# Chunked attention heads worked in eight steps of two chunks instead of sixteen of one

## The chip, the cores and the metric

One core of one Trainium2 chip runs the whole kernel. The metric is the device time of one execution in microseconds (us), the median of several runs. The profile was taken of one execution.

## The reference, cut to what matters

One layer on 1024 tokens of width 1024, all in float32:

```python
h = rmsnorm(x, pre_g)
p = h @ w_in                       # q, k, v, gate of group A and of group B
ya = sliding_window_sink_attention(aq, ak, av, sinks) * silu(ag)
yb = differential_attention(bq, bk, bv, lam, lambda_init, subln_g) * silu(bg)
y = concat(ya, yb) @ w_out
return x + rmsnorm(y, post_g)
```

Group A has 8 query heads and 2 key/value heads of 64. Tokens lie in 16 chunks of 64, and a chunk's queries see the keys of their own chunk and of the one before (64 queries by 128 keys). A linear bias in the distance is added, a learned sink takes part in the softmax, and the weights multiply the values. Group B has 4 heads with two softmax maps each; it is swept in blocks of 128 queries over all earlier keys, and the second map is subtracted with a factor before the values.

## The kernel before, in words

All order is written out by `make_schedule` (line 103). It makes one list of named steps, and each engine's program walks the list and does its own part of a step; so the place of a name in the list is the order on every engine's queue, and semaphores join the queues. After a preamble (normalise, transpose, project all values) the list is made of 51 slots: 24 units of group B (heads 0 to 2, eight query blocks each, unit names b0 to b23), 16 of group A (one for each chunk), the last 8 of B (b24 to b31), and 3 slots that finish. In a slot stand the scores of one unit and the transpose and values of an earlier one: one slot earlier for B, two for A (line 142). Between them stand pieces of the input projection. `PIECES_BESIDE` (line 85) says how many to a slot. A piece is 4 matmuls of 512 columns; six pieces make a half of a projection unit (128 output columns by 512 tokens). When a half is done, ACT stores it (`store`), and DVE makes what belongs to it: low parts for the q and k of B (`store_low`), the gate product (`gate`). Two units ahead of a unit's first piece, its weights are split (`split`): ACT writes the rounded part w_hi (line 711), POOL the rest w_lo (line 622). One piece is always taken behind the values (line 197), whatever the number says.

A chunk c goes through these steps. `a_scores` on PE (line 1228) is four matmuls, each for a pair of heads, on 64 rows of the array, into one of two sets of PSUM banks; on DVE (line 1044) four reductions that add the bias, write `a_weights` and take the row's minimum, then the sink's argument (line 1049); on ACT (line 820) four exponentials with row sums, then the sink's (line 823). `a_weights` on DVE (lines 1055, 1058) is the total and its reciprocal, on POOL (line 676) the multiply with it. `a_transpose` is four transposes on PE (line 1236) into the bank `turned`, which the B units use too, and ACT's copy (line 831). `a_values` is two matmuls on PE (line 1246), which fill half of the bank `mixed`, and DVE's scaled copy into `qT_A` (line 1063). The buffers `a_weights` hold two chunks and share their place with `weights_1` of B.

`SCORES_FIRST` and `PIECE_BETWEEN` (lines 89, 90) name slots in which the scores stand ahead of the transposes, or a piece between the two. In a B unit, DVE mixes the two maps (`b_mix`, line 1000), PE transposes (line 1194), ACT copies (line 792), PE multiplies with the values (line 1204).

Of the kernel before, what the change touches and what calls it, by code (L numbers as in the profile page):

```python
# [31 lines left out]
P = 128  # L32
# [12 lines left out]
CHUNKS = SEQ // CHUNK  # L45
HALF = 512
# [56 lines left out]
def make_schedule():  # L103
# [33 lines left out]
    order = [("b", u) for u in range(3 * TILES)] + [("a", c) for c in range(CHUNKS)]  # L137
# [3 lines left out]
    for unit, n in place.items():  # L141
        turns.setdefault(n + (1 if unit[0] == "b" else 2), []).insert(0, unit)
# [80 lines left out]
def hybrid_layer(nc, x, w_in, w_out, pre_norm_g, post_norm_g, sinks, lambda_q1, lambda_k1,  # L223
# [27 lines left out]
    a_weights = place("a_weights", 148.25, [P, 2, A_PAIRS, P])  # L251
    a_weightsT = place("a_weightsT", 152.25, [P, A_PAIRS, P])
# [15 lines left out]
    small = place("small", 206.25, [P, 352])  # L268
# [17 lines left out]
    def column(width):  # L286
        taken[0] += width
        assert taken[0] <= 352
        return small[:, taken[0] - width:taken[0]]
# [12 lines left out]
    min_a = column(2 * A_PAIRS)  # L302
    sum_a = column(2 * A_PAIRS)
    sink_arg = column(2 * A_PAIRS)
    sink_w = column(2 * A_PAIRS)
    total_a = column(2 * A_PAIRS)
    inv_a = column(2 * A_PAIRS)
# [110 lines left out]
    def a_scores_at(c, j):  # L418


        return 1024 * (c % 2) + 512 * (j // 2) + P * (j % 2)
# [112 lines left out]
    with nc.Block() as block:  # L534
# [83 lines left out]
        def _(pool):  # L618
# [35 lines left out]
            for step, *i in SCHEDULE:  # L654
# [16 lines left out]
                elif step == "a_weights":  # L671
                    c = i[0]
                    pool.wait_ge(a_inverted, c + 1)
                    w = a_weights[:, c % 2]
                    r = inv_a[:, 4 * (c % 2):4 * (c % 2) + 4].unsqueeze(2).to_broadcast([P, A_PAIRS, P])
# [7 lines left out]
        def _(act):  # L683
# [53 lines left out]
            for step, *i in SCHEDULE:  # L737
# [46 lines left out]
                elif step == "b_transpose":  # L784
# [4 lines left out]
                    if u == 3 * TILES:  # L789
                        act.wait_ge(a_valued, CHUNKS)  # L790
# [23 lines left out]
                elif step == "a_scores":  # L814
                    c = i[0]
                    s = 4 * (c % 2)
                    for j in range(A_PAIRS):
                        w = a_weights[:, c % 2, j, :]
                        act.wait_ge(a_biased, 4 * c + j + 1)
                        nc.scalar.activation(w, w, ACT.Exp, scale=-1.0, bias=min_a[:, s + j:s + j + 1],  # L820
                                             accum_out=sum_a[:, s + j:s + j + 1]).then_inc(a_exped, 1)
                    act.wait_ge(a_sinked, c + 1)
                    nc.scalar.activation(sink_w[:, s:s + 4], sink_arg[:, s:s + 4], ACT.Exp).then_inc(a_exped, 1)
                elif step == "a_transpose":
                    c = i[0]
                    if c:
                        act.wait_ge(a_valued, c)
# [3 lines left out]
                    nc.scalar.activation(a_weightsT[:, :, :], turned[:, :].rearrange("p (j q) -> p j q", q=P),  # L831
# [30 lines left out]
        def _(dve):  # L862
# [80 lines left out]
            for step, *i in SCHEDULE:  # L943
# [20 lines left out]
                elif step == "gate":  # L964
# [13 lines left out]
                    else:  # L978
                        dve.wait_ge(mixed_read, mixed_users.index(("a_values", CHUNKS - 1)) + 1)
# [22 lines left out]
                elif step == "b_scores":  # L1002
# [7 lines left out]
                    if u == 3 * TILES:  # L1010
                        dve.wait_ge(turned_full, turned_count("a_transpose", CHUNKS - 2))
                    if u == 3 * TILES + 2:
# [20 lines left out]
                elif step == "a_scores":  # L1033
                    c = i[0]
                    s = 4 * (c % 2)
                    if c == 0:
# [3 lines left out]
                    if c >= 2:  # L1040
                        dve.wait_ge(turned_full, turned_count("a_transpose", c - 2))
                    dve.wait_ge(a_scored, c + 1)
                    for j in range(A_PAIRS):
                        nc.vector.tensor_tensor_reduce(  # L1044
                            out=a_weights[:, c % 2, j, :], in0=scores[:, a_scores_at(c, j):a_scores_at(c, j) + P],
                            in1=dist_a[:, min(c, 1), :], scale=neg_slope[:, j:j + 1], scalar=neg_sink[:, j:j + 1],
                            op0=ALU.add, op1=ALU.min, accum_out=min_a[:, s + j:s + j + 1]).then_inc(a_biased, 1)
                    dve.wait_ge(a_biased, 4 * c + 4)
                    nc.vector.tensor_tensor(sink_arg[:, s:s + 4], min_a[:, s:s + 4], neg_sink,
                                            ALU.subtract).then_inc(a_sinked, 1)  # L1050
                elif step == "a_weights":
                    c = i[0]
                    s = 4 * (c % 2)
# [5 lines left out]
                elif step == "a_values":  # L1059
                    c = i[0]  # L1060
                    dve.wait_ge(a_valued, c + 1)

                    nc.vector.tensor_scalar(qT_A[:, :, c],
                                            mixed[:, 0:A_PAIRS * CHUNK].rearrange("p (r s q) -> p r s q", s=2, q=CHUNK),
# [34 lines left out]
        def _(pe):  # L1099
# [51 lines left out]
            for step, *i in SCHEDULE:  # L1151
# [63 lines left out]
                elif step == "a_scores":  # L1215
                    c = i[0]
                    if c == 0:
# [4 lines left out]
                    if c >= 2:  # L1222
                        pe.wait_ge(a_biased, A_PAIRS * (c - 1))
                    for j in range(A_PAIRS):
                        part = slice(HEAD_DIM * (j // 2), HEAD_DIM * (j // 2 + 1))
                        at = a_scores_at(c, j)
                        pair = qT_A[part, j % 2, c].rearrange("p s q -> p (s q)")
                        last = nc.tensor.matmul(scores[:, at:at + P], pair, kT_A[part, CHUNK * c:CHUNK * c + P],  # L1228
                                                start=True, stop=True)
                    last.then_inc(a_scored, 1)  # L1230
                elif step == "a_transpose":
# [3 lines left out]
                    for j in range(A_PAIRS):  # L1235
                        last = nc.tensor.transpose(turned[:, P * j:P * j + P], a_weights[:, c % 2, j, :],  # L1236
                                                   ident[:, :])
                    last.then_inc(turned_full, 1)
                elif step == "a_values":
                    c = i[0]  # L1240
                    pe.wait_ge(turned_read, turned_count("a_transpose", c))
                    pe.wait_ge(mixed_read, mixed_before((step, *i)))
                    for h in range(2):
                        part = slice(HEAD_DIM * h, HEAD_DIM * (h + 1))
                        v = v_sb[:, c // 2, B_WIDTH:V_WIDTH] if c % 2 else v_shift[:, c // 2, :]
                        last = nc.tensor.matmul(mixed[part, 0:A_PAIRS * CHUNK], v[:, part],  # L1246
                                                a_weightsT[:, 2 * h:2 * h + 2, :], start=True, stop=True)
# [37 lines left out]
```

## Time and profile before

| | |
|---|---|
| median of 3 runs | 531.47 us (531.39 to 532.06) |
| span of the profiled execution | 529.6 us |
| PE busy | 511.7 us (97%) |
| DVE busy | 269.9 us (51%) |
| ACT busy | 250.5 us (47%) |
| POOL busy | 105.8 us (20%) |
| mean granted clock of PE | 0.997 of full speed |

The span runs from the first to the last instruction; the profiled execution has no time of its own beside it, and the median of the runs is 1.87 us above it. Engines: PE is the matrix engine (its weight loads are listed as PEld), DVE the vector engine, ACT the scalar engine, POOL GpSimd. Lines such as L1164 are lines of the kernel. Matmuls are pipelined, so their printed lengths overlap; where the time of a group is wanted, it is read from its start to the start of the next.

### The profile page before, as it was taken

What the parts mean: (1) busy time and instruction counts of PE and PEld (TensorE: products, weight loads), DVE (VectorE), ACT (ScalarE), POOL (GpSimd) and SP (SyncE); (2) the same over time, 40 slices, a digit from 0 to 9 for tenths busy, and PEclk for the clock granted to TensorE, in tenths of its full rate; (3) what the DMA queues carried; (4) which work ended last, traced back from release to release, by engine and by line L of the source; (5) the groups of instructions that cost most, each with busy time, mean ns of one, the idle gap of its engine ahead of it and who ended that gap; (6) DMA issues with size and microseconds to landing.
All of it is one profiled execution on the core that took longest, in us unless ns stands there. A gap on an engine that the chain in (4) does not pass through costs nothing.

```text
span 529.6 us, 7514 instructions
## 1 busy us (share of the span) xinstructions
PE 511.7 (97%) x2776; PEld 424.8 (80%) x2776; DVE 269.9 (51%) x650; ACT 250.5 (47%) x614; POOL 105.8 (20%) x91
## 2 busy tenths in 40 slices
PE   6899999999999999999988999999999999999995
PEld 6799997888878887888875666678788887888884
DVE  3656002465675566445446687656555385443332
ACT  5454213466476466556565675644454463221211
POOL 3410303030112110212033243222201252000000
PEclk9999999999999999999999999999999999999998
DMA  8730005130101110110111010111000653332222
GB/s 295 228 123 2 1 15 143 41 74 6 40 10 33 40 41 0 41 40 9 34 41 27 14 41 1 40 41 41 0 1 0 144 176 120 102 132 84 80 79 79
DMA packets 41300, 32.57 MB, mean 61 GB/s; under 512 B 18544, under 2 KB 35888, under 8 KB 41264
## 3 DMA queue, kind: packets, MB, share of 16 engines
q1 hardware_dynamic: 38960, 27.89, 18.7%
q10 hardware_dynamic: 2304, 4.20, 2.1%
q8 instruction: 22, 0.36, 0.3%
q14 instruction: 14, 0.11, 0.1%
HBM read 27.40 MB, written 4.19 MB: 60 GB/s over the span
## 4 chain that ended last, share of the span: by engine, by line
PE 85%; ACT 4%; DVE 4%; issue 3%; DMA 2%; POOL 2%; SPq 0%; DVEq 0%; POOLq 0%; ACTq 0%
PE proj L1164 39%; PE scores L1263 14%; PE proj L1134 10%; PE scores L1183 7%; PE banks L1204 6%; PE banks L1194 3%; PE scores L1228 2%; PE banks L1246 2%; PE banks L1236 1%; PE scores L1107 1%; DVE k_stack L961 1%; DMA pre_g<-in_pre_norm_g 1%; DMA w_raw<-in_w_in 1%; ACT k_stack L762 1%; PE banks L1213 1%
## 5 line engine op out<-in xcount | busy, mean ns | idle before, releaser
L1164 PE MATMUL proj<-hT_hi,w_hi 128*128 128x512 f32 x336 | 90.0, 401 | 0.8 <-DVE k_stack L961 0.6
L1164 PE MATMUL proj<-hT_lo,w_hi 128*128 128x512 f32 x336 | 90.6, 402 | 0.0
L622 POOL TENSOR_TENSOR w_lo<-w_raw,w_hi 128x1024 fp32r<-128x1024 f32 x21 | 51.0, 2430 | 195.4 <-ACT w_hi L711 195.4
L1164 PE MATMUL proj<-hT_hi,w_lo 128*128 128x512 f32 x336 | 89.2, 400 | 0.0
L1164 PEld LDWEIGHTS proj<-hT_hi,w_hi 128*128 128x128 f32 x336 | 60.3, 188 | 15.0 <-issue 1.9
L1164 PEld LDWEIGHTS proj<-hT_hi,w_lo 128*128 128x128 f32 x336 | 60.8, 188 | 13.7 <-issue 1.9
L1164 PEld LDWEIGHTS proj<-hT_lo,w_hi 128*128 128x128 f32 x336 | 59.9, 188 | 13.2 <-issue 1.9
L1016 DVE CUSTOM_DVE_ANT_0 weights<-scores,dist_b 128x128 f32<-128x128 f32 (+7 forms) x64 | 45.9, 755 | 47.2 <-PE scores L1183 47.0
L782 ACT ACTIVATE weights<-weights,small 128x128 f32<-128x128 f32 (+7 forms) x64 | 49.0, 767 | 14.0 <-DVE small L1016 14.0
L792 ACT ACTIVATE weightsT<-banks 128x512 f32<-128x512 f32 (+3 forms) x48 | 23.5, 490 | 51.4 <-PE banks L1194 51.4
L1183 PE MATMUL scores<-k_stack,q_stack 128*128 128x512 f32 (+3 forms) x192 | 41.9, 353 | 0.0
L1204 PEld LDWEIGHTS banks<-v_sb,weightsT 128*128 128x128 f32 x288 | 36.3, 191 | 5.8 <-ACT weightsT L792 3.2
L1204 PE MATMUL banks<-v_sb,weightsT 128*128 128x128 f32 x288 | 37.8, 276 | 1.1 <-ACT weightsT L792 1.1
L1183 PEld LDWEIGHTS scores<-k_stack,q_stack 128*128 128x128 f32 x192 | 31.9, 189 | 4.8 <-DVE k_stack L961 0.4
L1000 DVE SCALAR_TENSOR_TENSOR weights<-weights,small,weights 128x512 f32<-128x512 f32 (+3 forms) x48 | 34.4, 745 | 1.1
L851 ACT ACTIVATE banks<-scores 128x512 f32<-128x512 f32 x16 | 9.3, 582 | 53.3 <-PE scores L1263 53.3
L626 POOL TENSOR_TENSOR small<-small 128x1 f32<-128x1 f32 (+1 forms) x24 | 16.9, 704 | 82.7 <-DVE small L1084 81.4
L1263 PE MATMUL scores<-wo_hi,hT_hi 128*128 128x512 f32 x128 | 32.0, 391 | 0.1
L820 ACT ACTIVATE a_weights<-a_weights,small 128x128 f32<-128x128 f32 x64 | 24.9, 391 | 14.7 <-DVE small L1044 14.6
L1263 PE MATMUL scores<-wo_hi,hT_lo 128*128 128x512 f32 x128 | 31.6, 389 | 0.0
L1263 PE MATMUL scores<-wo_lo,hT_hi 128*128 128x512 f32 x128 | 31.6, 389 | 0.0
L961 DVE TENSOR_TENSOR k_stack<-proj,k_stack 64x512 fp32r<-64x512 f32 x32 | 22.0, 688 | 15.6 <-ACT k_stack L762 14.8
(106 smaller groups left out, 724.7 us busy)
## 6 DMA issues: line engine op xcount, KB each, us to landing
w_raw<-in_w_in SPq DMA_DIRECT2D x13, 512.0 KB, 3.9
x_in<-in_x SPq DMA_DIRECT2D x8, 512.0 KB, 5.5
w_raw<-in_w_in SPq DMA_DIRECT2D x16, 256.0 KB, 3.6
x_res<-in_x SPq DMA_DIRECT2D x8, 512.0 KB, 4.4
out<-y_out ACTq DMA_DIRECT2D x16, 256.0 KB, 2.2
wv_raw<-in_w_in SPq DMA_DIRECT2D x2, 640.0 KB, 7.4
wo_early<-in_w_out SPq DMA_DIRECT2D x4, 256.0 KB, 4.5
w_raw<-in_w_out SPq DMA_DIRECT2D x4, 256.0 KB, 6.5
```

The costliest lines, as they stand in the source:

```text
L622: nc.gpsimd.tensor_tensor(w_lo[:, n % SPLIT], w_raw[:, n % RAW], w_hi[:, n % SPLIT].bitcast(F32), ALU.subtract).then_inc(w_lo_ready, 1)
L782: nc.scalar.activation(w, w, ACT.Exp, scale=-1.0, bias=min_b[:, 2 * u + m:2 * u + m + 1], accum_out=sum_b[:, 2 * u + m:2 * u + m + 1]).the ...
L792: nc.scalar.activation(weightsT[:, 4 * r:4 * r + blocks, :], turned[:, 0:P * blocks].rearrange("p (b q) -> p b q", q=P), ACT.Copy).then_in ...
L820: nc.scalar.activation(w, w, ACT.Exp, scale=-1.0, bias=min_a[:, s + j:s + j + 1], accum_out=sum_a[:, s + j:s + j + 1]).then_inc(a_exped, 1)
L961: nc.vector.tensor_tensor(k_lo[part, m, tokens], source[own, :], k_hi[own, m, tokens].bitcast(F32), ALU.subtract).then_inc(stack_lo, 1)
L1000: nc.vector.scalar_tensor_tensor(w0, w1, mix_b[:, u:u + 1], w0, ALU.mult, ALU.add).then_inc(b_mixed, 1)
L1016: nc.vector.tensor_tensor_reduce(out=weights_1[:, 0:keys] if m else weights_0[:, u % 2, 0:keys], in0=scores[:, 1024 * m:1024 * m + keys], ...
L1134: last = nc.tensor.matmul(proj[:, n % 2, 0:VG], h[:, k, tokens], w[:, k, cols], start=(p == 0 and k == 0), stop=(p == PASSES - 1 and k == ...
L1164: last = nc.tensor.matmul(to, w[:, slot, k, :], h[:, k, HALF * half:HALF * half + HALF], start=(p == 0 and k == first), stop=(p == PIECES ...
L1183: last = nc.tensor.matmul(scores[:, 1024 * m + first:1024 * m + first + width], q_stack[head][m][:, P * block_:P * block_ + P], k[:, m, fi ...
L1204: last = nc.tensor.matmul(mixed[:, P * (u % 4):P * (u % 4) + P], weightsT[:, b, :], v_sb[:, b, P * head:P * head + P], start=(b == 0), sto ...
L1263: last = nc.tensor.matmul(scores[:, at:at + HALF], y[:, k, tokens], w[:, k, cols], start=(p == 0 and k == 0), stop=(p == PASSES - 1 and k ...
```

## The change

The A heads are worked in 8 steps p of the chunks 2p and 2p+1. One step of scores makes both chunks' scores (8 matmuls) and signals once. The transposes stay one for each chunk: 2p at the start of step p+1, 2p+1 after the next scores and one piece. The values of both chunks are one step (4 matmuls) and fill the whole bank `mixed`, and DVE copies them at once. The lag between scores and values is one step instead of two. ACT's exponentials become steps of their own (`a_exp`) and stand after the transposes' copies. The small columns and the `a_weights` and `a_weightsT` buffers are doubled. The numbers of pieces in the slots change, from `[5,3,3,1,1,4,3,4,3,2,2,4,3,2,3,2]` to `[8,6,6,6,6,6,6,6]` for A and by one less in five later slots.

```diff
 PIECES_BESIDE = ([9, 4, 3, 4, 4, 5, 3, 7] + [5, 5, 2, 3, 6, 5, 2, 8] + [5, 5, 3, 4, 3, 5, 3, 6]
-                 + [5, 3, 3, 1, 1, 4, 3, 4, 3, 2, 2, 4, 3, 2, 3, 2]
-                 + [4, 7, 7, 6, 3, 6, 5, 5] + [6, 1, 5])
-
-SCORES_FIRST = {1, 2, 3, 10, 11, 17, 18, 45}
-PIECE_BETWEEN = {16, 27, 31, 44, 45}
-A_BEFORE = 1
+                 + [8, 6, 6, 6, 6, 6, 6, 6]
+                 + [4, 6, 6, 5, 3, 6, 5, 4] + [5, 1, 5])
+
+SCORES_FIRST = {1, 2, 3, 10, 11, 17, 18, 37}
+PIECE_BETWEEN = {16, 36, 37}
...
-    order = [("b", u) for u in range(3 * TILES)] + [("a", c) for c in range(CHUNKS)]
+    order = [("b", u) for u in range(3 * TILES)] + [("a", p) for p in range(STEPS_A)]
...
-        turns.setdefault(n + (1 if unit[0] == "b" else 2), []).insert(0, unit)
+        turns.setdefault(n + 1, []).insert(0, unit)
...
         if last[0] == "a":
-            steps.append(("a_weights", last[1]))
+            steps.append(("a_weights", 2 * last[1] + 1))
         turning = sorted(turns.get(slot, []))
-        first = [(f"{which}_transpose", unit, 0) if which == "b" else ("a_transpose", unit)
+        first = [("b_transpose", unit, 0) if which == "b" else ("a_transpose", 2 * unit)
...
-            now_taken = min(count, A_BEFORE) if kind == "a" and which == "a" else 1 + finishing
+            if which == "a":
+                take(1)
+                count -= 1
+                if kind == "a":
+                    steps.append(("a_exp", 2 * now))
+                steps.append(("a_transpose", 2 * unit + 1))
+            now_taken = 2 if which == "a" else 1 + finishing
             take(now_taken)
             count -= now_taken
+            if kind == "a":
+                if which == "b":
+                    steps.append(("a_exp", 2 * now))
+                steps += [("a_exp", 2 * now + 1), ("a_weights", 2 * now)]
             steps.append((f"{which}_values", unit))
...
-    a_weights = place("a_weights", 148.25, [P, 2, A_PAIRS, P])
-    a_weightsT = place("a_weightsT", 152.25, [P, A_PAIRS, P])
+    a_weights = [place("a_weights0", 148.25, [P, 2, A_PAIRS, P]), place("a_weights1", 144.25, [P, 2, A_PAIRS, P])]
+    a_weightsT = place("a_weightsT", 152.25, [P, 2, A_PAIRS, P])
...
-        return 1024 * (c % 2) + 512 * (j // 2) + P * (j % 2)
+        return 1024 * (c // 2 % 2) + 512 * (j // 2) + 2 * P * (c % 2) + P * (j % 2)
...
                 elif step == "a_scores":
-                    c = i[0]
...
+                    if p >= 2:
+                        pe.wait_ge(a_biased, 2 * A_PAIRS * (p - 1))
+                    for c in (2 * p, 2 * p + 1):
+                        for j in range(A_PAIRS):
+                            part = slice(HEAD_DIM * (j // 2), HEAD_DIM * (j // 2 + 1))
+                            at = a_scores_at(c, j)
+                            pair = qT_A[part, j % 2, c].rearrange("p s q -> p (s q)")
+                            last = nc.tensor.matmul(scores[:, at:at + P], pair, kT_A[part, CHUNK * c:CHUNK * c + P],
+                                                    start=True, stop=True)
                     last.then_inc(a_scored, 1)
...
                 elif step == "a_values":
-                    c = i[0]
-                    pe.wait_ge(turned_read, turned_count("a_transpose", c))
+                    p = i[0]
+                    pe.wait_ge(turned_read, turned_count("a_transpose", 2 * p + 1))
                     pe.wait_ge(mixed_read, mixed_before((step, *i)))
...
+                    for e in range(2):
+                        v = v_sb[:, p, B_WIDTH:V_WIDTH] if e else v_shift[:, p, :]
+                        to = mixed[:, 256 * e:256 * e + 256]
+                        for h in range(2):
+                            part = slice(HEAD_DIM * h, HEAD_DIM * (h + 1))
+                            last = nc.tensor.matmul(to[part, :], v[:, part], a_weightsT[:, e, 2 * h:2 * h + 2, :],
+                                                    start=True, stop=True)
                     last.then_inc(a_valued, 1)
```

On DVE, `a_scores` does the eight reductions and two sink arguments of both chunks one after the other, having waited once for both chunks' scores; `a_values` is one copy of 512 columns where there were two of 256.

## Rows read from the trace of the kernel before

**Rows 1.** The page: span, and busy time of each engine.
```profile
span 529.6 us, 7514 instructions
PE 511.7 (97%) x2776; PEld 424.8 (80%) x2776; DVE 269.9 (51%) x650; ACT 250.5 (47%) x614; POOL 105.8 (20%) x91
```

**Rows 2.** PE's waits by releaser (total us, times, longest), and its timeline at b23.
```profile
PE banks L1246 <- DVE qT_A L1063: 1.4, 1, 1.4
PE banks L1204 <- ACT weightsT L792: 1.1, 1, 1.1
PE banks L1236 <- POOL a_weights L676: 0.3, 1, 0.3
...
266.03 0.63 PE L1194 MATMUL banks<-ident,weights 128*128 128x128 f32 x4 [0.30 <-ACT weightsT L792]
```

**Rows 3.** Timeline of PE over one chunk (start us, length us, line, out<-in).
```profile
321.74 0.60 PE L1236 MATMUL banks<-ident,a_weights 128*128 128x128 f32 x4
322.27 0.72 PE L1228 MATMUL scores<-kT_A,qT_A 64*128 64x128 f32 x8
322.92 1.20 PE L1164 MATMUL proj<-hT_hi,w_lo 128*128 128x512 f32 x4
324.05 0.65 PE L1246 MATMUL banks<-a_weightsT,v_sb 128*64 128x256 f32 x4
324.63 1.20 PE L1164 MATMUL proj<-hT_hi,w_lo 128*128 128x512 f32 x4
325.66 1.98 PE L1164 MATMUL proj<-hT_hi,w_hi 128*128 128x512 f32 x8
327.49 0.60 PE L1236 MATMUL banks<-ident,a_weights 128*128 128x128 f32 x4
```

**Rows 4.** Timeline of PE where a piece follows a transpose.
```profile
283.10 0.60 PE L1236 MATMUL banks<-ident,a_weights 128*128 128x128 f32 x4
283.45 1.18 PE L1164 MATMUL proj<-hT_hi,w_hi 128*128 128x512 f32 x4
```

**Rows 5.** Timeline of PE, the first two records of a values group.
```profile
334.65 0.44 PE L1246 MATMUL banks<-a_weightsT,v_sb 128*64 128x256 f32 x2
```

**Rows 6.** Timeline of the other engines over the chunk of rows 3.
```profile
321.93 1.04 POOL L676 TENSOR_TENSOR a_weights<-a_weights,small 128x512 f32<-128x512 f32 x1 [1.93 <-DVE small L1058]
...
322.44 0.60 ACT L831 ACTIVATE a_weightsT<-banks 128x512 f32<-128x512 f32 x1 [0.99 <-PE banks L1236]
...
323.16 0.41 DVE L1044 CUSTOM_DVE_ANT_0 a_weights<-scores,dist_a,small 128x128 f32<-128x128 f32 x1 [1.31 <-PE scores L1228]
...
323.62 0.40 ACT L820 ACTIVATE a_weights<-a_weights,small 128x128 f32<-128x128 f32 x1 [0.58 <-DVE small L1044]
...
324.62 0.16 DVE L1049 TENSOR_TENSOR small<-small 128x4 f32<-128x4 f32 x1
...
325.17 0.19 ACT L823 ACTIVATE small<-small 128x4 f32<-128x4 f32 x1
```

**Rows 7.** Timeline of ACT, DVE and POOL around a k store and a split.
```profile
296.32 2.44 ACT L762 ACTIVATE k_stack<-proj 64x512 fp32r<-64x512 f32 x4 [0.50 <-PE proj L1164]
298.79 2.85 DVE L961 TENSOR_TENSOR k_stack<-proj,k_stack 64x512 fp32r<-64x512 f32 x4 [3.16 <-ACT k_stack L762]
...
325.86 0.60 ACT L775 ACTIVATE gate<-proj 128x512 f32<-128x512 f32 x1 [0.50 <-PE proj L1164]
326.36 1.05 ACT L711 ACTIVATE w_hi<-w_raw 128x1024 fp32r<-128x1024 f32 x1
327.49 2.65 POOL L622 TENSOR_TENSOR w_lo<-w_raw,w_hi 128x1024 fp32r<-128x1024 f32 x1 [4.52 <-ACT w_hi L711]
327.82 2.33 DVE L1055 TENSOR_TENSOR small<-small 128x4 f32<-128x4 f32 x1
```

**Rows 8.** Timeline of DVE and PE at the mix of unit b26.
```profile
363.94 2.25 DVE L1000 SCALAR_TENSOR_TENSOR weights<-weights,small,weights 128x384 f32<-128x384 f32 x1
...
366.55 0.49 PE L1194 MATMUL banks<-ident,weights 128*128 128x128 f32 x3
```

More of the change, by code:

```diff
@@ L45 @@
 CHUNKS = SEQ // CHUNK
+STEPS_A = CHUNKS // 2
 HALF = 512
@@ L267, in hybrid_layer @@
     junk = place("junk", 205.75, [P, P])
-    small = place("small", 206.25, [P, 352])
+    small = place("small", 206.25, [P, 392])
     wv_raw = place("wv_raw", 120, [P, KT, V_WIDTH])
@@ L287, in column @@
         taken[0] += width
-        assert taken[0] <= 352
+        assert taken[0] <= 392
         return small[:, taken[0] - width:taken[0]]
@@ L301, in hybrid_layer @@
     scale_b = column(4)
[L302 to L307, printed above, removed]
+    min_a = column(4 * A_PAIRS)
+    sum_a = column(4 * A_PAIRS)
+    sink_arg = column(4 * A_PAIRS)
+    sink_w = column(4 * A_PAIRS)
+    total_a = column(4 * A_PAIRS)
+    inv_a = column(4 * A_PAIRS)
     neg_half = column(4)
@@ L418, in a_scores_at, with a_weights_of @@
     def a_scores_at(c, j):
-        return 1024 * (c % 2) + 512 * (j // 2) + P * (j % 2)
+        return 1024 * (c // 2 % 2) + 512 * (j // 2) + 2 * P * (c % 2) + P * (j % 2)
+    def a_weights_of(c):
+        return a_weights[c // 2 % 2][:, c % 2]
     def y_parts(t, to):
@@ L673, in _ @@
                     pool.wait_ge(a_inverted, c + 1)
-                    w = a_weights[:, c % 2]
-                    r = inv_a[:, 4 * (c % 2):4 * (c % 2) + 4].unsqueeze(2).to_broadcast([P, A_PAIRS, P])
+                    w = a_weights_of(c)
+                    r = inv_a[:, 4 * (c % 4):4 * (c % 4) + 4].unsqueeze(2).to_broadcast([P, A_PAIRS, P])
                     nc.gpsimd.tensor_tensor(w, w, r, ALU.mult).then_inc(a_weighted, 1)
@@ L789, in _ @@
                     if u == 3 * TILES:
-                        act.wait_ge(a_valued, CHUNKS)
+                        act.wait_ge(a_valued, STEPS_A)
                     act.wait_ge(turned_full, turned_count("b_transpose", u, r))
@@ L813, in _ @@
                                          ACT.Copy, scale=out_g).then_inc(turned_read, 1)
-                elif step == "a_scores":
+                elif step == "a_exp":
                     c = i[0]
-                    s = 4 * (c % 2)
+                    s = 4 * (c % 4)
                     for j in range(A_PAIRS):
-                        w = a_weights[:, c % 2, j, :]
+                        w = a_weights_of(c)[:, j, :]
                         act.wait_ge(a_biased, 4 * c + j + 1)
@@ L825, in _ @@
                     c = i[0]
-                    if c:
-                        act.wait_ge(a_valued, c)
+                    if c >= 2:
+                        act.wait_ge(a_valued, c // 2)
                     else:
@@ L978, in _ @@
                     else:
[L979 removed]
+                        dve.wait_ge(mixed_read, mixed_users.index(("a_values", STEPS_A - 1)) + 1)
                     nc.vector.tensor_tensor(o, by_chunk(gate[:, :]), o, ALU.mult).then_inc(gated, 1)
@@ L1010, in _ @@
                     if u == 3 * TILES:
-                        dve.wait_ge(turned_full, turned_count("a_transpose", CHUNKS - 2))
-                    if u == 3 * TILES + 2:
+                        dve.wait_ge(turned_full, turned_count("a_transpose", CHUNKS - 3))
+                    if u == 3 * TILES + 1:
                         dve.wait_ge(turned_full, turned_count("a_transpose", CHUNKS - 1))
@@ L1043, in _ @@
[L1043 to L1048, printed above, removed]
@@ L1049, in _ @@
-                    nc.vector.tensor_tensor(sink_arg[:, s:s + 4], min_a[:, s:s + 4], neg_sink,
-                                            ALU.subtract).then_inc(a_sinked, 1)
+                    elif p == 1:
+                        dve.wait_ge(turned_full, turned_count("b_transpose", 3 * TILES - 1, 1))
+                    else:
+                        dve.wait_ge(turned_full, turned_count("a_transpose", 2 * p - 3))
+                    dve.wait_ge(a_scored, p + 1)
+                    for c in (2 * p, 2 * p + 1):
+                        s = 4 * (c % 4)
+                        for j in range(A_PAIRS):
+                            nc.vector.tensor_tensor_reduce(
+                                out=a_weights_of(c)[:, j, :],
+                                in0=scores[:, a_scores_at(c, j):a_scores_at(c, j) + P],
+                                in1=dist_a[:, min(c, 1), :], scale=neg_slope[:, j:j + 1],
+                                scalar=neg_sink[:, j:j + 1], op0=ALU.add, op1=ALU.min,
+                                accum_out=min_a[:, s + j:s + j + 1]).then_inc(a_biased, 1)
+                        dve.wait_ge(a_biased, 4 * c + 4)
+                        nc.vector.tensor_tensor(sink_arg[:, s:s + 4], min_a[:, s:s + 4], neg_sink,
+                                                ALU.subtract).then_inc(a_sinked, 1)
@@ L1051, in _ @@
                 elif step == "a_weights":
                     c = i[0]
-                    s = 4 * (c % 2)
+                    s = 4 * (c % 4)
                     dve.wait_ge(a_exped, 5 * c + 5)
@@ L1059, in _ @@
                 elif step == "a_values":
-                    c = i[0]
-                    dve.wait_ge(a_valued, c + 1)
-                    nc.vector.tensor_scalar(qT_A[:, :, c],
-                                            mixed[:, 0:A_PAIRS * CHUNK].rearrange("p (r s q) -> p r s q", s=2, q=CHUNK),
+                    p = i[0]
+                    dve.wait_ge(a_valued, p + 1)
+                    nc.vector.tensor_scalar(qT_A[:, :, 2 * p:2 * p + 2].rearrange("p r c s q -> p r c (s q)"),
+                                            mixed.rearrange("p (c r x) -> p r c x", c=2, r=2),
                                             0.5, None, ALU.mult).then_inc(mixed_read, 1)
@@ L1215, in _ @@
                 elif step == "a_scores":
-                    c = i[0]
-                    if c == 0:
+                    p = i[0]
+                    if p == 0:
                         pe.wait_ge(pads_made, 2)
@@ L1221, in _ @@
                         pe.wait_ge(b_biased, 2 * 3 * TILES)
[L1222 to L1229, printed above, removed]
+                    if p >= 2:
+                        pe.wait_ge(a_biased, 2 * A_PAIRS * (p - 1))
+                    for c in (2 * p, 2 * p + 1):
+                        for j in range(A_PAIRS):
+                            part = slice(HEAD_DIM * (j // 2), HEAD_DIM * (j // 2 + 1))
[3 more added lines that the diff above has]
+                                                    start=True, stop=True)
                     last.then_inc(a_scored, 1)
@@ L1235, in _ @@
                     for j in range(A_PAIRS):
-                        last = nc.tensor.transpose(turned[:, P * j:P * j + P], a_weights[:, c % 2, j, :],
+                        last = nc.tensor.transpose(turned[:, P * j:P * j + P], a_weights_of(c)[:, j, :],
                                                    ident[:, :])
@@ L1239, in _ @@
                 elif step == "a_values":
-                    c = i[0]
-                    pe.wait_ge(turned_read, turned_count("a_transpose", c))
+                    p = i[0]
+                    pe.wait_ge(turned_read, turned_count("a_transpose", 2 * p + 1))
                     pe.wait_ge(mixed_read, mixed_before((step, *i)))
[L1243 to L1247, printed above, removed]
+                    for e in range(2):
[5 more added lines that the diff above has]
+                                                    start=True, stop=True)
                     last.then_inc(a_valued, 1)
```

8 lines of the change are left out of this document (2 added, 6 removed).

## The prediction

> **What bounds the kernel now.** I read the page's shares first: PE is busy 97% of the span, no other engine more than about half [rows 1]. The span is 529.6 us; the runs' median of 531.47 us lies 1.87 us above it, which I take for what lies around the span and keep unchanged. Then the waits of PE, by line. In the stretch of the A units (264 to 354 us) PE stands still only four times: 0.30 us before the second transpose of unit b23, 1.07 us before b23's values, 1.38 us before the values of chunk 2 and 0.27 us before the transpose of chunk 5 [rows 2]; together 3.0 us. So a change here can win only what PE itself does less, plus these 3.0 us, and can lose whatever new waits it makes. Then PE's timeline of one chunk [rows 3], read from start to start, since the printed lengths overlap. T is a transpose group (4 records), S a scores group (8), V a values group (4), P one projection piece (4 matmuls). T starts at 321.74, S at 322.27, P at 322.92, V at 324.05, P at 324.63, two more P at 325.66, the next T at 327.49. So T takes 0.53 ahead of S, S 0.65, P between S and V 1.13, V 0.58, P after V 1.03, and each P among P's 1.83 / 2 = 0.915. Ahead of a P a transpose takes 0.35 [rows 4]. The same piece costs 0.1 more behind a group of another kind and 0.1 more ahead of S or V: changes of kind cost PE time, and the change makes fewer of them.
>
> **PE's own time.** No matmul, transpose or byte is added or removed; 16 transpose groups stay 16, but 16 scores groups become 8 of double size (S') and 16 values groups 8 (V'). A chunk now, with two pieces: 0.53 + 0.65 + 1.13 + 0.58 + 1.03 = 3.92; with three, 4.84. Two chunks with six pieces: 9.67 us.
> A new step with six pieces runs T S' P T P P V' P P P. S' adds 8 records to 8: these stand 0.45 / 7 = 0.064 apart (0.72 less the 0.27 of one), so 0.45 to 0.51 more; I take 0.45, giving 1.10. V' adds two pairs: two records end at 0.44 and four at 0.65, a pair every 0.21 [rows 5, 3], so 0.42 more, giving 1.00. The sum: T 0.53, S' 1.10, P 1.03, T 0.35, P 1.01, P 1.01, V' 1.00, P 1.03, P P 1.83 = 8.89. That is 0.78 less per step. Seven full steps give 5.5; S'(0) and V'(7), which stand alone at the two ends, 0.2 and 0.4; from that go 0.2 for the few transposes that already precede a piece. **PE saves 5.9 us.** If a half of S' and V' still cost as much as a whole group does now (0.65 and 0.58), the step saves only 0.78 - 0.20 - 0.16 = 0.42 and the whole 3.4 us; that is the lower bound. The upper is 6.5, if V's later records follow at 0.08 apart.
> On just this the Trainium skill speaks (TensorEngine Tiling (Array Packing), Key Properties): changing the tiling mode drains the engine, another tile of the same mode does not. The rows show S and V on part of the array (64*128, 128*64) and P on all of it, and the dearer P beside them; that the inside of a double group is free of it, no row shows. By the rule the term is 5.9, by whole groups 3.4.
>
> **The pieces.** The plan gives 45, 43 and 12 pieces to the A units, the last B units and the end; afterwards 50, 39 and 11. Two A slots that are listed with one piece take two, because a piece is always taken after the values, so it is really 47 before. All pieces are done in either case; no DMA is added or moved but by the slot in which a weight split stands. Cost: nothing, as long as the B units stay covered (third rival).
>
> **The old waits.** The 0.30 and 1.07 were b23's second copy on ACT waiting behind chunk 0's exponentials; the exponentials now come after both b23 copies, so both go. The 1.38 (DVE held up ahead of a values copy) and the 0.27 go with their order. That is 3.0 us won; nothing else was late within them.
>
> **The new waits.** One step of lag: chunks 2p and 2p+1 are scored in step p and transposed in step p+1, at its start and 2.7 us later (0.53 + 1.10 + 1.03). A full step, with 0 at its first transpose, goes as follows [rows 6]. S' ends its issue at 1.63; the first reduction on DVE starts 0.24 behind the next P's start, 1.9. Four of them and the sink argument take 1.46 + 0.16; so chunk 2p is reduced by 3.5 and 2p+1 by 5.1. ACT's exponentials start 0.46 behind DVE: four take 1.55 and the sink's 0.19, done by 4.1. Then comes the copy of the second transpose (0.60), done at 4.7; V' is due at 0.53 + 1.10 + 1.03 + 0.35 + 2.02 = 5.0. PE is not held, but the margin is only 0.3.
> The sum and reciprocal of 2p and POOL's multiply (1.04) end by 6.7, due at 8.9. For 2p+1 the exponentials stand on ACT behind the store of the half projection that ends just before V' (every sixth piece, and the steps are of six). Its ready time is about 5.3, then the store: 0.60 for a gate, 2.44 for a k (four copies), so 1.2 for a q (two) [rows 7]; then exponentials of 1.7. With a gate they end at 7.7. That alone is in time for 8.89 + 2.7 = 11.6.
> But in every other step the next weight split stands just behind (steps 1, 3, 5 and 7): w_hi 1.05 on ACT, then w_lo 2.4 on POOL (2.65 in the row, whose start overlaps a DVE product), which is in order, ahead of the multiply of 2p+1. With a gate: 7.7 + 1.0 + 2.4 = 11.1, plus 1.04 = 12.15, against 11.6: 0.55 late. And DVE's sum (two inputs from SBUF) does not move while w_lo runs: 2.33 us instead of 0.16 [rows 7]. One wait per transposed second chunk:
> - T(3), behind step 1 (a q store and w_lo): DVE's sum comes as w_lo starts, so sum, reciprocal and multiply follow it. 0.9 late.
> - T(5), behind step 2 (a k store, no split): the low parts on DVE take 2.85 from 7.8 [rows 7], then the sum, reciprocal and multiply to 12.2. 0.6 late.
> - T(7), behind step 3 (a k store and w_lo): exponentials to 9.5, w_hi to 10.5, w_lo to 12.9, then 0.4 and 1.04: 14.35. 2.75 late, the largest.
> - T(9) and T(13), steps without split: none.
> - T(11): 0.6. T(15): its step has a B scores group in place of S', so it is due at 10.75: 1.4.
> **New waits 6.25 us.** Lower bound 2: what of each wait is left if the sums of T(3) and T(7) get through before w_lo and the k low parts overlap the exponentials. Upper bound 9, if each of the four split steps loses what T(7) does less its k parts (about 1.8) and V' is held too for 0.2 a step.
>
> **The sum.** -5.9 - 3.0 + 6.25 = -2.65 us: a span of 526.9 and a time of 528.8 us.
>
> **Rivals.**
> (a) The new waits stay near their lower bound of 2 us. For it: DVE's sum is 0.16 long and slips in before w_lo if it comes a little earlier than I place it, and a wait at one transpose gives slack to the next. Against it: POOL is in order, and w_lo stands ahead of the multiply whatever DVE does. -5.9 - 3.0 + 2.2 = -6.7: 524.8 us.
> (b) Double groups save only by the bound of whole groups, 3.4. For it: each S pairs its matmuls on two halves of the array, and a new pair might wait. Against it: the even spacing inside the groups [rows 3, 5]. -3.4 - 3.0 + 6.25 = -0.15: 531.3 us, no change.
> (c) Slower: the cover taken from the last B units is missed. Five of their slots lose a piece of 0.915. A B unit's mix must be done when its transpose comes one slot later; where the margin is under 0.9, the transpose waits. At unit 26 it is 0.36: the mix runs from 363.94 for 2.25 and the transpose starts at 366.55 [rows 8]. If all five slots fall short as a whole, 5 x 0.915 = 4.6, -2.65 + 4.6 = +1.9: 533.4 us. It decides from three slots on. Against it: the 2.25 falls beside a w_lo again, as in rows 7, and the splits now stand at other places; the other mixes end over a microsecond ahead in the timeline. I count nothing for it in the sum.
> (d) The tight 0.3 at V' is missed in every step. It is missed if ACT's copy comes behind more than I put ahead of it; each 0.3 beyond costs 8 x 0.3 = 2.4, and so 531.2.
>
> **How the numbers follow.** The forecast 0.45, (a) 0.22, (b) 0.11, (c) 0.12, (d) 0.10. A measurement here tells about 0.2%, 1.06 us, from no change. Faster: all of the forecast but 0.04, all of (a), a third of (b) and (d): 0.70. Same: 0.04 of the forecast, half of (b) and (d), a little of (c): 0.16. Slower: most of (c) and the rest: 0.14. The range goes from (a) with another microsecond of its waits gone, 523.8, to just past (b) and (d), 532.0. Under 2 in 10 lie outside: no waits at all, and (c).
>
> **What would show it.** In the profile after, S' from start to the next P at 1.10 and V' at 1.00 show the first term; 1.30 and 1.16 show (b). PE's waits in the A steps: at the transposes, released by POOL's multiply, some 6 us in five places, with the one of chunk 7 the longest, and none at the values. Waits at the values released by ACT's copy show (d); waits at the transposes of units 25 to 31, released by DVE's mix, (c). PE's busy time should fall by less than the saved 5.9, since the printed length of a group reaches into the time lost ahead of the next. I am wrong if the store, the exponentials and the split do not stand in that order on ACT, or if POOL's multiply comes ahead of w_lo.

## Result and profile after

The changed kernel takes 533.52 us (median of 9 runs, 531.83 to 535.51) against 531.57 us (9 runs, 531.10 to 532.08): ratio 1.0038, interval 1.0022 to 1.0053. It is slower by about 2 us, and its single runs lie 3.7 us apart where those of the kernel before lie 1.0 apart. One run of over 1000 us in each of two experiments, and one of the kernel before, are left out of every range here. The profiled execution took 533.66 us with a span of 531.9 (the kernel before: 529.6, [rows 1]).

The page after, span and busy time:
```profile
span 531.9 us, 7491 instructions
PE 508.7 (96%) x2776; PEld 427.0 (80%) x2776; DVE 263.0 (49%) x642; ACT 250.7 (47%) x614; POOL 105.0 (20%) x91
```
PE is busy 3.0 us less and the span is 2.3 us longer: PE waits more. The waits of PE by releaser, which answer to [rows 2] (total us, times, longest):
```profile
PE banks L1256 <- POOL a_weights L690: 3.3, 3, 2.2
...
PE banks L1213 <- DVE weights L1014: 2.4, 2, 1.8
...
PE scores L1285 <- DVE hT_lo L1090: 1.5, 1, 1.5
...
PE banks L1232 <- DVE on_b L1044: 0.6, 1, 0.6
```
The first is the expected one, at the transposes (L1256). The others are new: the transpose of unit b24 behind DVE's mix (1.8 of the 2.4; the other 0.7 was there before), and two at the end of the projection. The four waits of [rows 2] (3.4 us, start to start) are gone.

One full step without a wait in PE's timeline, which answers to [rows 3]:
```profile
335.95 0.60 PE L1256 MATMUL banks<-ident,a_weights 128*128 128x128 f32 x4
336.48 1.26 PE L1248 MATMUL scores<-kT_A,qT_A 64*128 64x128 f32 x16
337.67 1.19 PE L1183 MATMUL proj<-hT_lo,w_hi 128*128 128x512 f32 x4
338.70 0.60 PE L1256 MATMUL banks<-ident,a_weights 128*128 128x128 f32 x4
339.05 2.09 PE L1183 MATMUL proj<-hT_hi,w_lo 128*128 128x512 f32 x8
341.07 0.65 PE L1268 MATMUL banks<-a_weightsT,v_shift 128*64 128x256 f32 x4
341.55 0.60 PE L1268 MATMUL banks<-a_weightsT,v_sb 128*64 128x256 f32 x4
342.08 2.14 PE L1183 MATMUL proj<-hT_hi,w_hi 128*128 128x512 f32 x8
344.06 1.08 PE L1183 MATMUL proj<-hT_lo,w_hi 128*128 128x512 f32 x4
344.98 0.60 PE L1256 MATMUL banks<-ident,a_weights 128*128 128x128 f32 x4
```
Start to start the step takes 344.98 - 335.95 = 9.03 us; the double scores group 1.19, the double values group 1.01. Two chunks with six pieces took 9.67.

Around the transpose of chunk 7, PE, POOL and DVE:
```profile
306.18 2.37 POOL L636 TENSOR_TENSOR w_lo<-w_raw,w_hi 128x1024 fp32r<-128x1024 f32 x1 [4.24 <-ACT w_hi L725]
306.42 2.15 DVE L1074 TENSOR_TENSOR small<-small 128x4 f32<-128x4 f32 x1
306.60 1.19 PE L1183 MATMUL proj<-hT_lo,w_hi 128*128 128x512 f32 x4
...
308.86 1.04 POOL L690 TENSOR_TENSOR a_weights<-a_weights,small 128x512 f32<-128x512 f32 x1 [0.32 <-DVE small L1077]
...
309.95 1.12 PE L1256 MATMUL banks<-ident,a_weights 128*128 128x128 f32 x4 [2.16 <-POOL a_weights L690]
310.72 3.17 PE L1183 MATMUL proj<-hT_hi,w_lo 128*128 128x512 f32 x8
313.82 0.65 PE L1268 MATMUL banks<-a_weightsT,v_shift 128*64 128x256 f32 x4
```
The wait is as foretold. What was not: the two pieces behind it take 313.82 - 310.72 = 3.10 us and not 2.02 (341.07 - 339.05), and the transposes 0.77 and not 0.35. The busy time by stretch shows why (the number behind POOL's is the granted clock of PE):
```profile
305.00:310.00 5.00, 2.84 (x26) 2.03 (x24) 4.87 (x11) 2.43 (x8) 3.41 (x2) 0.96 0.02 4
310.00:312.00 2.00, 2.00 (x7) 1.81 (x8) 1.93 (x13) 1.61 (x8) 0.00 (x0) 0.50 1.15 246
312.00:314.00 2.00, 2.00 (x8) 1.29 (x9) 0.20 (x2) 0.07 (x1) 1.04 (x1) 0.74 0.05 7
314.00:316.00 2.00, 2.00 (x13) 1.30 (x12) 1.05 (x2) 2.00 (x10) 0.00 (x0) 1.00 0.00 0
```
The clock stood at half, 1.2 GHz, from the end of PE's idle to 313, and at full speed, 2.4 GHz, on both sides. It cost 1.08 us in the pieces and 0.42 in the transposes, about 1.5 us, on top of the wait.

**The account**, from the first transpose of b23 to the end of b24's values: 264.48 to 354.12 before, 264.91 to 355.99 after. The changed kernel does 55 pieces in it and the kernel before 53, so two pieces of 0.915 are added there: 91.5 us before, 91.1 after. Of the 91.5, 3.4 are waits. Of the 91.1, 6.2 are: 0.4 behind the first double values group, 0.3 at chunk 5, 2.3 at chunk 7, 0.1 at chunk 11, 1.0 at chunk 15, 1.9 at b24, 0.2 scattered; and 1.5 more are the low clock. The rest is 83.4 against 88.1: **PE's own work became 4.7 us shorter**. All that is used up by b24. From there to the output projection the changed kernel loses 2.6 us more. The stretches ahead of and behind these two hold the same work in both; in these executions they differ by +0.4 and -0.3.

### The profile page after: what moved, and what is told of

Its sections match the earlier page's. It is cut to its first block, busy times and chain, and to the rows that moved or that the text cites. A ratio compares the mean times of both kernels' runs of the same rounds, so it can differ in the third digit from the quotient of the medians.

```text
span 531.9 us, 7491 instructions
## 1 busy us (share of the span) xinstructions
PE 508.7 (96%) x2776; PEld 427.0 (80%) x2776; DVE 263.0 (49%) x642; ACT 250.7 (47%) x614; POOL 105.0 (20%) x91
## 4 chain that ended last, share of the span: by engine, by line
PE 77%; DVE 6%; issue 6%; ACT 4%; POOL 3%; DMA 3%; SPq 0%; DVEq 0%; POOLq 0%; ACTq 0%
PE proj L1183 33%; PE scores L1285 14%; PE proj L1153 10%; PE scores L1202 6%; PE banks L1223 5%; PE banks L1213 3%; DVE k_stack L975 2%; PE scores L1248 1%; ACT k_stack L776 1%; PE banks L1256 1%; PE scores L1126 1%; DMA w_raw<-in_w_in 1%; DMA pre_g<-in_pre_norm_g 1%; POOL w_lo L636 1%; PE banks L1268 1%
## 5 line engine op out<-in xcount | busy, mean ns | idle before, releaser
L1183 PEld LDWEIGHTS proj<-hT_hi,w_lo 128*128 128x128 f32 x336 | 62.0, 191 | 11.9
L796 ACT ACTIVATE weights<-weights,small 128x128 f32<-128x128 f32 (+7 forms) x64 | 49.0, 767 | 12.8 <-DVE small L1030 12.7
L1014 DVE SCALAR_TENSOR_TENSOR weights<-weights,small,weights 128x512 f32<-128x512 f32 (+3 forms) x48 | 32.8, 711 | 1.1
L1061 DVE CUSTOM_DVE_ANT_0 a_weights<-scores,dist_a,small 128x128 f32<-128x128 f32 x64 | 22.5, 407 | 16.5 <-PE scores L1248 16.4
L1285 PEld LDWEIGHTS scores<-wo_hi,hT_hi 128*128 128x128 f32 x128 | 24.0, 188 | 6.9 <-DVE hT_lo L1090 2.0
```

Source lines behind the costliest of these rows:

```text
L796: nc.scalar.activation(w, w, ACT.Exp, scale=-1.0, bias=min_b[:, 2 * u + m:2 * u + m + 1], accum_out=sum_b[:, 2 * u + m:2 * u + m + 1]).the ...
L1014: nc.vector.scalar_tensor_tensor(w0, w1, mix_b[:, u:u + 1], w0, ALU.mult, ALU.add).then_inc(b_mixed, 1)
L1061: nc.vector.tensor_tensor_reduce(out=a_weights_of(c)[:, j, :], in0=scores[:, a_scores_at(c, j):a_scores_at(c, j) + P], in1=dist_a[:, min(c ...
L1183: last = nc.tensor.matmul(to, w[:, slot, k, :], h[:, k, HALF * half:HALF * half + HALF], start=(p == 0 and k == first), stop=(p == PIECES ...
L1285: last = nc.tensor.matmul(scores[:, at:at + HALF], y[:, k, tokens], w[:, k, cols], start=(p == 0 and k == 0), stop=(p == PASSES - 1 and k ...
```

## Experiments

All are timed beside the kernel before in the same job. The three jobs were on different chips; the changed kernel itself gave 534.59 us, ratio 1.0056 (1.0040 to 1.0071), in the first.

**The changed kernel again** (and once more in the third job: 534.98 us, 1.0052).

> The changed kernel again, as the base for the others. If its time is settled by fixed waits, it lies at about 533.5 us with a spread as narrow as the kernel before (0.5 us); if a clock drop that comes in some executions and not in others has part in it, single runs spread over 530 to 535.5 and follow the mean clock.

Six runs from 532.8 to 535.86; the spread is the kernel's own. In the second repeat the fastest run (531.87) has a mean granted clock of 0.999 and the five others (533.88 to 535.30) 0.986 to 0.992; in the first repeat time and clock go together only loosely.

**The split behind the multiply.**
```diff
             if half == 0 and p == 0 and n + 2 < NU:
-                steps.append(("split", n + 2))
+                (put_off if holding[0] else steps).append(("split", n + 2))
...
             steps.append(("a_weights", 2 * last[1] + 1))
+            steps += put_off
+            put_off.clear()
+        holding[0] = kind == "a"
```


> Only change: in the A steps the weight split (w_hi, w_lo) stands in the list behind the sum and multiply of chunk 2p+1, so POOL does the multiply first. Theory 1 (POOL's order makes the long waits): the wait at the transpose of chunk 7 falls from 2.2 us to under 0.4, that of chunk 15 from 0.9 to nothing, and the slow stretch behind chunk 7, which takes some 1.4 us more than the same pieces elsewhere, goes with it: 533.5 - 1.9 - 0.9 - 1.4 = 529.3, and a narrow spread. Rival (DVE's low parts of k are what is late): chunk 7's wait stays above 1.5 us and the time above 532.

530.77 us, ratio 0.9976 (0.9966 to 0.9986): 3.8 us less than the changed kernel beside it. PE's waits on POOL in this kernel:
```profile
PE banks L1260 <- POOL a_weights L694: 0.4, 2, 0.2
```
From 3.3 us to 0.4, so POOL's order made the long waits, not DVE's low parts. A wait of 0.6 for ACT's copy came at the values of chunk 7's step in their place. But single runs still lie from 528.65 to 531.13, and in the profiled one the clock fell behind another wait, that for b24's mix:
```profile
349.66 0.48 PE L1217 MATMUL banks<-ident,weights 128*128 128x128 f32 x1 [1.76 <-DVE weights L1018]
349.79 1.20 PE L1206 MATMUL scores<-k_stack,q_stack 128*128 128x256 f32 x4
350.79 1.91 PE L1187 MATMUL proj<-hT_hi,w_hi 128*128 128x512 f32 x4
352.50 0.63 PE L1227 MATMUL banks<-v_sb,weightsT 128*128 128x128 f32 x2
```
The piece takes 1.71 us to the next start. In the changed kernel's profile it took 0.93 behind the same wait of 1.76, at full clock.

**b24's mix first.**
```diff
+            if which == "a" and kind == "b":
+                steps.append(("b_mix", now))
             steps.append((f"{which}_values", unit))
```
(and it is left out at its old place).

> Only change: DVE mixes unit b24 ahead of the copy of the last A values and of the gate product, not behind them. Theory: the wait of 1.8 us at the first transpose of b24 goes, no other wait takes its place: 1.8 us less than the changed kernel (about 531.7). Rival: PE stops at the next thing in line (b24's values, waiting for ACT's copy) for over a microsecond, and under 0.8 us is won.

531.26 us, ratio 0.9987 (0.9977 to 0.9998): 3.3 us less than the changed kernel, more than the wait of 1.9. The rest is not shown; a low clock behind this wait in some executions, as in the profile above, would fit. PE goes straight on:
```profile
351.17 1.20 PE L1185 MATMUL proj<-hT_hi,w_hi 128*128 128x512 f32 x4
352.20 0.27 PE L1215 MATMUL banks<-ident,weights 128*128 128x128 f32 x1
352.23 0.72 PE L1204 MATMUL scores<-k_stack,q_stack 128*128 128x256 f32 x4
```
In the changed kernel it stood as follows:
```profile
346.96 0.19 ACT L796 ACTIVATION_READ_ACCUMULATOR weights<-weights,small 128x1 f32 x1
...
351.43 0.69 DVE L1082 TENSOR_SCALAR qT_A<-banks 128x512 f32<-128x512 f32 x1 [4.99 <-PE banks L1268]
352.04 0.68 DVE L987 SCALAR_TENSOR_TENSOR gate<-gate,proj 128x512 f32<-128x512 f32 x1
352.75 0.69 DVE L994 TENSOR_TENSOR out_B<-gate,out_B 128x512 f32<-128x512 f32 x1
...
353.87 0.35 DVE L1014 SCALAR_TENSOR_TENSOR weights<-weights,small,weights 128x128 f32<-128x128 f32 x1
...
354.27 0.33 PE L1213 MATMUL banks<-ident,weights 128*128 128x128 f32 x1 [1.76 <-DVE weights L1014]
```
The wait was one of order: DVE stood idle for 5.0 us until the A values were there, and then had their copy (0.69), the gate product and the gating (0.68, 0.69) ahead of a mix whose inputs had been ready for six microseconds.

**The two pieces put back.**
```diff
-                 + [4, 6, 6, 5, 3, 6, 5, 4] + [5, 1, 5])
+                 + [4, 6, 6, 5, 3, 6, 5, 5] + [6, 1, 5])
```


> Only change: the two pieces that the late slots have lost against the kernel before are put back (102 pieces beside the units instead of 100, as the kernel before really has). Theory (the plan of the end shifted): the wait of 0.6 us at the last finish transpose and the 1.5 us ahead of the output projection both go, 2.1 to 2.5 us less than the changed kernel. Rival (the output weights simply landed late in the profiled execution, which is chance): the profile shows the same wait or none, but the times of the rounds fall by less than 0.8 us.

531.04 us, ratio 0.9989 (0.9976 to 1.0001): 3.6 us less than the changed kernel, and the waits of 0.6 and 1.5 us are not in its profile. Here too more is won than the 2.1 us of the waits, and where the rest comes from is not shown.

**The same two pieces taken from the kernel before.**
```diff
-                 + [4, 7, 7, 6, 3, 6, 5, 5] + [6, 1, 5])
+                 + [4, 7, 7, 6, 3, 6, 5, 4] + [5, 1, 5])
```


> The kernel before with one part of the change alone: the two late slots give up a piece each, so 100 pieces stand beside its units and 19 are left for the end. Theory (those two pieces are the whole loss at the end: 0.6 us at the last finish transpose, 1.5 us ahead of the output projection): 2.0 to 2.5 us slower than before. Rival (the loss at the end needs something else of the change): under 0.8 us slower.

534.01 us (533.47 to 534.33), ratio 1.0043 (1.0031 to 1.0055): 2.4 us slower with nothing else of the change. Its profile has the two waits:
```profile
PE scores L1263 <- DVE hT_lo L1071: 1.5, 1, 1.5
...
PE banks L1213 <- DVE on_b L1030: 0.6, 1, 0.6
```

**The output weights' splits at their old pieces.**
```diff
-        if outs and at % OUT_EVERY == 0:
+        if outs and at >= 236 and at % OUT_EVERY == 0:
```


> The changed kernel with its 100 pieces, and only the splits of the output weights held back to the pieces at which the kernel before has them (the first at piece 236). Theory (these splits, two pieces earlier, stand ahead of the last gate's product on DVE and POOL and delay the first low part of y): the wait of 1.3 to 1.5 us ahead of the output projection goes, the 0.6 us at the finish transpose stays: 1.4 us and more less than the changed kernel. Rival (the missing cover of two pieces makes both): the wait ahead of the output projection stays above 1 us.

532.09 us, ratio 1.0005 (0.9993 to 1.0017), against 1.0038 to 1.0056 for the changed kernel. In its profile the 1.5 is gone and the 0.6 is left. So the missing cover (the two pieces that now come later) makes only the 0.6; the 1.5 is order. With 19 pieces left instead of 17, each output split stands two pieces earlier. In the changed kernel one on POOL then lies beside DVE's last gating ahead of y's first part:
```profile
433.80 2.40 POOL L674 TENSOR_TENSOR wo_lo<-w_raw,wo_hi 128x1024 fp32r<-128x1024 f32 x1 [1.17 <-ACT wo_hi L758]
...
434.35 2.40 DVE L994 TENSOR_TENSOR out_B<-gate,out_B 128x512 f32<-128x512 f32 x1
...
437.29 0.76 DVE L1090 TENSOR_TENSOR hT_lo<-qT_A,hT_hi 128x256 fp32r<-128x256 f32 x2 [0.54 <-ACT hT_hi L855]
```
The gating takes 2.40 us where 0.69 is usual. This is [rows 7] again: the Trainium skill (SBUF — State Buffer, Who interferes with whom) has it that a DVE instruction with two inputs in SBUF and a GpSimd one that reads SBUF hold the shared port in turn, each to its end. The trace agrees: DVE ended 0.55 us behind POOL, a little less than a product's own 0.69.

**PE kept busy in chunk 7's wait.**
```diff
+                    if c == 7:
+                        for _ in range(20):
+                            nc.tensor.transpose(turned[:, 0:P], ident[:, :], ident[:, :])
                     pe.wait_ge(a_weighted, c + 1)
```


> The changed kernel, with 20 further transposes of the identity on PE into the free bank ahead of the wait for chunk 7's multiply; PE is busy in that wait instead of idle, and nothing else moves. Theory (the slow stretch behind chunk 7 is the clock's answer to the idle): the granted clock is full behind chunk 7, the pieces there take 2.0 us a pair and not 3.1, and the time is 1.2 to 1.6 us less than the changed kernel. Rival (the stretch is slow for another reason, as the accesses of ACT and DVE to PSUM): no change, or 0.3 us more if the transposes outlast the wait.

533.37 us, ratio 1.0027 (1.0016 to 1.0038). The stretch behind it in its profile:
```profile
307.53 2.35 PE L1256 MATMUL banks<-ident 128*128 128x128 f32 x20
309.87 0.66 PE L1259 MATMUL banks<-ident,a_weights 128*128 128x128 f32 x4
310.29 2.09 PE L1183 MATMUL proj<-hT_hi,w_lo 128*128 128x512 f32 x8
312.31 0.65 PE L1271 MATMUL banks<-a_weightsT,v_shift 128*64 128x256 f32 x4
```
The same two pieces take 2.02 us, not 3.10, with POOL, ACT and DVE at the same work, and the granted clock is full there. So the slow stretch followed from the idle, and not from the other engines. The ratio falls by only 0.0011 to 0.0029 (0.6 to 1.5 us, where 1.2 to 1.6 was expected), and the runs still lie 2.0 us apart; the next experiment takes that up.

**PE kept busy in three waits** (also 16 transposes ahead of b24's mix and 13 ahead of the output projection).

> The changed kernel, with further transposes of the identity on PE not only ahead of chunk 7's multiply (20) but also in the waits for b24's mix (16) and for the first low part of y (13). All waits keep their length, PE is only not idle in them. Theory (each of the three idles can be followed by a stretch at the low clock, about 1.4 us each, the first in every execution, the others in some): the spread over the runs shrinks from 3 to 4 us to about 1, and the median is 1.5 to 3 us under the changed kernel's, with the granted clock full in 300 to 440 us. Rival (the spread comes from elsewhere, as the landing of transfers): the spread stays, and only the 1.4 us of chunk 7 is won.

532.18 us, 11 runs within 1.05 us (531.73 to 532.78), ratio 1.0010 (1.0001 to 1.0018); the changed kernel beside it 534.98 with 3.4 us between its runs. 2.8 us of the median in this job (2.2 by the two ratios) are thus the low clock behind idles, and so is most of the spread. In the changed kernel's own profile in that job the clock had stayed full behind chunk 7's wait, and had fallen behind that at the output projection instead (the first 8 matmuls take 2.66 us to the next start, the third 8 take 1.81; 1.6 us are lost by it):
```profile
437.52 2.86 PE L1285 MATMUL scores<-wo_hi,hT_hi 128*128 128x512 f32 x8 [2.00 <-DVE hT_lo L1090]
440.18 2.87 PE L1285 MATMUL scores<-wo_hi,hT_lo 128*128 128x512 f32 x8
442.89 1.98 PE L1285 MATMUL scores<-wo_lo,hT_hi 128*128 128x512 f32 x8
```

**The three repairs together.** Split, mix and pieces as above.

> The three repairs together (split behind the multiply, b24's mix first, the two pieces back). The three waits lie in three stretches of PE's timeline, so if they only add up the gains do too: the waits removed are 2.8 (chunks 7 and 15), 1.8 and 2.1 us, 6.7 us, and the slow stretches behind them, so against the kernel before 0.990 to 0.985 (524 to 526 us), with a spread of about 1 us. Rival (one hides another): a wait moves and the ratio stays above 0.993.

524.90 us, four runs within 0.26 us, ratio 0.9871 (0.9858 to 0.9885), a span of 523.2 us: 6.8 us faster than the kernel before. No wait above 0.65 us is left in the A steps; a wait of 0.84 among the last B units (PE at 376.83) was there before (at 383.19).

**Values in two groups again, on top of the repairs.**
```diff
+            if which == "a":
+                take(1)
+                steps.append(("a_values_first", unit))
+                take(1)
```
(the first chunk's two matmuls, then a piece, then the second's).

> The three repairs, and the values of a step in two groups again, with a piece between them; the same matmuls. Theory (each further group of another kind costs PE time at its two edges, 0.36 us by the start-to-start times of the kernel before): 7 steps of 0.36, and 0.36 where the last one stands, 2.5 to 2.9 us slower than the three repairs alone. Rival (the group's edges are free, only waits count): within 0.6 us of it.

527.68 us (527.46 to 527.89), ratio 0.9924: 2.8 us slower than the repairs alone. In the profiles a full step without a wait takes 9.37 us instead of 9.04, and PE's waits in the A steps differ by only 0.2. The change's first term is real, and the share of the values in it is timed by itself: 8 groups more at 0.35 us each. The double scores groups were not undone.

## Why the prediction was wrong

It forecast 528.8 us and faster; the time is 533.5 and slower, outside its range. By its own steps:

- **PE's own time, -5.9.** The mechanism is shown, the size was off: 4.7 us (account above). The step takes 9.03 and not 8.89: the double scores group takes 1.19, between the 1.10 I took and the 1.30 of whole groups, and 0.05 came at the values and behind them. Record by record the sixteen matmuls keep the pace of the eight, a pair every 0.11 us, but for one slip of 0.10 at the twelfth, in all eight groups; why, no run shows. On the rule of the Trainium skill that the prediction cites (TensorEngine Tiling (Array Packing), Key Properties): the runs fit it, with 0.35 us for each further values group among pieces and no loss where the second chunk begins inside a double one; a drain itself no run shows.
- **Old waits, -3.0.** Right; 3.4 from start to start.
- **New waits, +6.25.** They came at the transposes I named, released by POOL, with chunk 7's longest. The size was 3.7: 2.3 there against 2.75, 1.0 at chunk 15 against 1.4, 0.3 at chunk 5 and 0.1 at chunk 11 against 0.6 each, and nothing at chunk 3 against 0.9. The walk of ACT and POOL was right within 0.3 us: counted from the first transpose of its step, POOL's multiply ended at 12.6, 12.1, 14.5, 11.9 and 11.9 us for chunks 3, 5, 7, 11 and 15, where I had 12.5, 12.2, 14.35, 12.15 and 12.15. What I had too early was PE. It came for these weights at 12.8, 11.8, 12.2, 11.8 and 10.9, and not at 11.6 (10.75 for chunk 15), since the steps are longer than 8.89 and a wait in one delays the next; the step that scored chunk 3 took 10.03, with a wait of 0.4 and four finish transposes of group B in it. That wait of 0.4, for the low parts of q behind the first double values group, I had not.
- **"The pieces ... Cost: nothing."** This step failed. The prediction had even counted that 47 pieces stood beside the A units, not 45, and then compared the plan's 100 with the true 102 as if nothing hung on it. Two pieces fewer beside the late units shift all that is placed by piece number at the end: 2.4 us, shown on the kernel before with nothing else changed.
- **Rival (c), counted at nothing.** At b26, where I saw the thin margin, nothing came. It came at b24, and not from lost cover: the last A values now come after both transposes, and DVE's list has their copy and a gate ahead of the mix. 1.9 us. The prediction walks ACT and POOL through that slot, and not DVE. That (c)'s 533.4 us stands beside the measured 533.5 is chance: it was the price of five slots short of cover, and what b24 waited for was the order on DVE, as its repair shows.
- **What no step had: the clock.** I priced a wait at its length. Behind an idle of 2.2 us PE mostly worked on at 1.2 GHz for about 3 us; over the three idles that is 2.8 us of the median in the third job.

In sum: -4.7 - 3.4 + 3.7 + 0.4 + 1.9 + 2.4 = +0.3, close to the +0.6 of the kernel with its three idles filled; and the 2.8 us of the clock on top make the +3.4 of that job (+2.0 in the first measurement). The likeliest case was right in kind for the A stage alone, -4.0 us without the clock, and there two misses worked against each other: PE saved 1.2 less than forecast, and the new waits came to 2.1 less. The 1.9 and the 2.4 behind the A stage used that up, and the clock made the kernel slower. That the merged steps pay once the order around them is mended, the repaired version shows.

## What to carry to other kernels

Where one list sets every engine's order, a change of how many pieces stand in one stage moves all later steps that are placed by count: list the last stage of both versions side by side before calling it untouched. In the slot where one kind of unit hands over to the next, walk every engine's queue, the one that seemed idle too. And price a wait of a busy PE above its length: behind waits of 1.8 to 2.2 us the low clock cost some 1.5 us more, in some executions here and in others not.

## What the runs showed of the hardware

The granted clock fell to half behind chunk 7's wait (PE idle for 2.2 us, at work before and after) in five of the six profiled executions that had it unfilled, to 0.50 to 0.52 in the lowest two microseconds. Behind b24's wait of 1.76 us it fell in one of seven; behind the wait at the output projection it fell once, at 2.0 us, and stayed full in the six that had 1.3 to 1.8 (one of them the kernel before without its two pieces). One such stretch costs about 1.5 us: 1.5 behind chunk 7, 1.6 at the output projection. The changed kernel's waits at chunk 7 and b24 were the same within 0.05 us in its three profiles, and that at the output projection 1.3, 1.5 and 2.0; its runs lie 3 to 4 us apart. With transposes into a free bank in the three waits they lie 1.05 apart. Which idles of 1.7 to 2.2 us are followed by the low clock, these runs do not tell.
